# The layout of the gates in DRAM: contiguous for the write or for the read

## What is computed

```python
s = jnp.einsum('thpc,hpkc->thpk', q, sub_keys).astype(jnp.float32)
top_s, top_i = lax.top_k(s, PEER_TOPK)
...
ids = i1 * N_KEYS + i2
g = jax.nn.softmax(best_s, axis=-1)
...
act = jax.nn.gelu(jnp.einsum('td,thkd->thk', xb, ue).astype(jnp.float32), approximate=False)
w = (g * act).astype(xb.dtype)
return jnp.einsum('thk,thkd->td', w, ve)
```

## Time and profile before

| | |
|---|---|
| median of three runs | 2915.62 us (2914.73 to 2916.62) |
| span of the profiled execution | 3018.1 us |
| mean granted TensorE clock | 0.968 |
| PE, DVE, POOL busy | 93%, 77%, 54% |
| DMA, whole span | 685.17 MB, 227 GB/s |

### The profile page before, as it was taken

The page is one execution under the profiler, slowest core; times in us unless marked ns, Lnnn a source line. Parts: engine busy times, 40 slices in busy tenths (PEclk is TensorE's granted clock), DMA queues, the critical chain, the costliest instruction groups (busy, mean ns, idle before and its releaser), DMA issues.

```text
span 3018.1 us, 33873 instructions
## 1 busy us (share of the span) xinstructions
PE 2813.2 (93%) x12016; PEld 2149.1 (71%) x12016; DVE 2333.2 (77%) x3821; ACT 965.7 (32%) x1335; POOL 1617.8 (54%) x1235
## 2 busy tenths in 40 slices
PE   7999699999799999999999999999999999999998
PEld 3546544788588888887777777777777777777776
DVE  2787952588998888886687878878787878788886
ACT  2014232211246656664222222223131313132232
POOL 1999400111023666664476667666666767676640
PEclk9999599999899999999999999999999999999999
DMA  3111010212457999999987888788877888787883
GB/s 120 42 42 56 1 42 1 84 43 84 167 168 233 324 326 335 346 342 361 387 314 264 295 271 295 276 287 291 278 274 265 287 281 288 259 318 278 315 293 147
DMA packets 253977, 685.17 MB, mean 227 GB/s; under 512 B 31984, under 2 KB 97648, under 8 KB 248432
## 3 DMA queue, kind: packets, MB, share of 16 engines
q0 software_dynamic: 104448, 335.81, 31.7%
q1 hardware_dynamic: 83568, 313.65, 29.0%
q10 hardware_dynamic: 65792, 33.56, 3.8%
HBM read 611.60 MB, written 71.30 MB: 226 GB/s over the span
## 4 chain that ended last, share of the span: by engine, by line
PE 42%; DVE 36%; DMA 7%; issue 7%; another core or an unknown queue 3%; DVEq 3%; POOL 1%; ACT 1%; SPq 0%; ACTq 0%; POOLq 0%
PE ps L1625 16%; DVE ps L1240 13%; DMA vring<-in_u_tab,idsA 6%; PE ps L1548 6%; PE ps L1590 5%; DVE hnT L922 4%; PE ps L1476 3%; DVE vl L1299 3%; DVE ul L1214 3%; PE ps L1617 3%; PE ps L1385 2%; DVE hg L1304 2%; DVE wl L1309 2%; DVE lx L1088 2%
## 5 line engine op out<-in xcount | busy, mean ns | idle before, releaser
L555 POOL DMA_INDIRECT vring<-in_v_tab,idsA x512 | 565.0, 1104 | 394.4 <-DVE ps L1240 214.8
L1240 DVE SCALAR_TENSOR_TENSOR ps<-vring,hsel,ps 128x1024 f32<-128x1024 f32 x508 | 652.5, 1284 | 24.6 <-DMA vring<-in_v_tab,idsA 5.8
L530 POOL DMA_INDIRECT hsel<-hidden,idsE x384 | 435.7, 1135 | 125.0 <-issue 114.0
L1625 PE MATMUL ps<-vh,wh 128*128 128x512 f32 x1024 | 410.7, 401 | 74.8 <-DVE wl L1309 66.9
L1625 PE MATMUL ps<-vh,wl 128*128 128x512 f32 x1024 | 409.3, 400 | 4.3 <-issue 4.3
L1617 PE MATMUL ps<-xh,ul 128*128 128x512 f32 x1024 | 406.8, 397 | 4.5 <-issue 4.5
L1617 PE MATMUL ps<-xh,uh 128*128 128x512 f32 x1024 | 406.5, 397 | 4.2 <-issue 3.1
L1617 PE MATMUL ps<-xl,uh 128*128 128x512 f32 x1024 | 405.6, 396 | 4.2 <-issue 3.9
L1625 PE MATMUL ps<-vl,wh 128*128 128x512 f32 x1024 | 407.1, 398 | 2.3 <-issue 2.3
L1316 DVE TENSOR_TENSOR acc<-acc,ps 128x512 f32<-128x512 f32 x256 | 175.0, 684 | 269.6 <-PE ps L1625 162.9
L864 ACT CAST vh<-v_raw 128x1024 fp32r<-128x1024 f32 x128 | 133.9, 1046 | 672.4 <-PE ps L1625 457.3
(11 more groups left out here) (188 smaller groups left out, 4833.3 us busy)
## 6 DMA issues: line engine op xcount, KB each, us to landing
xraw<-in_uX SPq DMA_DIRECT2D x128, 512.0 KB
u_raw<-in_uT SPq DMA_DIRECT2D x128, 512.0 KB
v_raw<-in_v_tab SPq DMA_DIRECT2D x128, 512.0 KB
gates<-gbuf ACTq DMA_DIRECT2D x16, 2048.0 KB
gt<-gates SPq DMA_DIRECT2D x32, 1024.0 KB
hidden<-hst SPq DMA_DIRECT2D x93, 256.0 KB
wqbuf<-in_w_q SPq DMA_DIRECT2D x16, 512.0 KB, 3.4
vring<-in_v_tab,idsA POOLq DMA_INDIRECT x512
```

Of the source, the lines that this page charges most:

```text
L530: nc.gpsimd.indirect_dma_start(out=hsel[:, n, k:k + 1], out_offset=None, in_=hidden_items, in_offset=bass.IndirectOffsetOnAxis(ap=idsE[:, ...
L555: nc.gpsimd.indirect_dma_start(out=vring[q % VS][:, :], out_offset=None, in_=v_rows, in_offset=bass.IndirectOffsetOnAxis(ap=idsA[:, n, k:k ...
L1240: nc.vector.scalar_tensor_tensor(out=bank2(6), in0=vring[slot][:, :], scalar=w, in1=bank2(6), op0=ALU.mult, op1=ALU.add).then_inc(cb_done, 1)
L1625: last = mm(ps[:, 2 + k % 4, :], w[:, c, tt * P:(tt + 1) * P], v[:, c, dh * 512:(dh + 1) * 512], start=c == 0 and w is wh and v is vh, sto ...
```

## The change

The order of the DRAM tensor becomes (set of 32 tokens, partition, block, token). The write of a full `gbuf` is then one run of 16 KB in each partition, and a group's read collects, for each partition, 16 pieces of 4 blocks x 32 tokens, 512 bytes each, that stand 2 MB apart. Bytes, number of transfers, queues, waits and the order of instructions stay as they are, and so does the layout of `gbuf` and `gt`.

```diff
-    gates = nc.dram_tensor("gates", (NG, P, HALF // SUB, GC, SUB), F32, kind="Internal").ap()
+    gates = nc.dram_tensor("gates", (HALF // SUB, P, NKEY, SUB), F32, kind="Internal").ap()
...
             def load_gates(g):
-                sp.dma_start(gt[:, :, :, :], gates[g]).then_inc(g_in, 16)
+                sp.dma_start(gt[:, :, :, :].rearrange("p m c t -> p m (c t)"),
+                             gates[:, :, g * GC:(g + 1) * GC, :].rearrange("m p c t -> p m (c t)")).then_inc(g_in, 16)
...
-                    act.dma_start(gates[:, :, m, :, :].rearrange("g p c t -> p g (c t)"),
-                                  gbuf[m % 2][:, :, :].rearrange("p (g c) t -> p g (c t)", c=GC)).then_inc(gates_out[m % 2], 16)
+                    act.dma_start(gates[m], gbuf[m % 2][:, :, :]).then_inc(gates_out[m % 2], 16)
```

## The result

The changed kernel takes 2948.48 us (median of four, 2944.36 to 2949.25), the kernel before 2916.12 on the same chip. The ratio is 1.0111, 95% interval 1.0097 to 1.0126. It is slower by 32 us, outside the forecast's range and on the other side.

What follows compares the result with a forecast made beforehand. DMA was taken as short in the write stage (98% busy), mostly hidden by PE's `xraw` buffers. - 8.1 - 1 + 1.1 = - 8.0 us gave 2915.6 - 8.0 = 2908 us, own range 2904 to 2914, overall 2888 to 2926.

Steps and rivals of the forecast that it cites:

- The prices: Engine time per piece: 616 ns for a 16 KB write piece, 27.9 ns for a 512-byte read piece.
- What of it reaches the end?: Write stage: of PE's 8.1 us waits for `lx` all are won, of 3.7 for `gbuf` 1; gain 9 us, bounds 0 to 11.8.
- Rival 3: Write stage: the write becomes a burst, `xraw` and gathered rows come 4.9 us late 13 times; + 15 us, 2931; chance 0.13.
- After a burst the engines are free for the others: Write stage, argument against the burst being slower: engines are free until the next write, some 30 us later.
- The sign that the forecast gave for it: Write stage: PE's waits for `lx` would come in runs of one per write if the burst made it slower.
- The extreme case drawn from it: Write stage: a write's eight pieces per engine pass in one turn, 4.9 us with nothing for the other queues.
- 18 us to spare: Later groups' reads: 3.6 us of work takes 9.8 us in place of 8, leaving 18 us before first use.
- Group 0's 1.1 us: Group 0's read, with `hidden` stores behind it that POOL's first gather awaits, is on the path: + 1.1 us (0 to 2.4).
- 2 us more fit in: Group 1's read ends by 1498 us for a use at 1506.23, so 2 us more cause no wait.
- Rival 1: Write stage: PE's wait was not DMA's doing, so only group 0's 1.1 us stays; 2917 (2913 to 2918); chance 0.28.
- rival 2: Write stage: DMA is the bound in the timed runs, so the whole 29 us saving counts; 2887 (or 2899); chance 0.18.
- rival 4: Groups: the read is late above 77 ns a piece, each 10 ns more costing 3.5 us a group; slower; chance 0.05.

Runs made afterwards that it cites:

- the kernel before, again: The kernel before with no edit, profiled a second time: span 2921.6 us, against 3018.1 us in its first profile.
- write's half alone: Against the kernel before: write in 16 KB runs as in the changed kernel, read in 8 KB runs, gates permuted; 2943.38 us, ratio 1.0087.

## Why the prediction was wrong

- **The prices were near.** A 16 KB piece 616 ns, measured 645. DMA share in the stage from 0.98 to about 0.92, measured 0.89. The reads' extra engine time was forecast at 21 to 35 us: queue 1's time went from 30.3% of 16 x 2921.6 us in the kernel before, again, to 31.6% of 16 x 2947.4, 738 us or 46 us of all engines, a third above the upper bound. An issue of the read went from 0.33 to 0.38 us, one of the write from 0.37 to 0.33.
- **The step that failed is "What of it reaches the end?"** It took PE's 8.1 + 3.7 us of waits as what a lighter DMA would give back, 8.1 + 1 in the sum. The lighter DMA did shorten ACT's wait for `xraw` from 990 to 1442, from 100.9 us in the kernel before, again, to 79.0; but in the same stretch PE's wait for `lx` went from 9.3 to 11.3 us, and the wait for `gbuf` from 1.5 to 16.1. The step treats 16 engines as one pool, where less work means earlier data for everybody. What decided was who is served while the write is under way: the write, with 76.5% of the engines for 6 us in the case shown, and SP's and POOL's transfers later. Gain 9 us forecast; loss measured 25 us (write's half alone, 1.0087) and 27 in the changed kernel's stage.
- **Rival 3, given a chance of 0.13, was the mechanism; its 24 us came near by luck.** 4.9 us x 13 x 0.38 = 24 us of waits, less 9 won, + 15. Measured: 13 us of waits more, nothing won, and 13.5 us more of PE's busy time, most of it from the clock, a term that no part of the sum had. Two remarks in it misled. "After a burst the engines are free for the others" is true (DMA share 0.71 from 1080 to 1090 in the changed kernel), but PE had 439.7 busy of 452 us and no room to make a lost wait good. And the names were only half right: `xraw` and gathered rows were named, while the chain runs through `xraw` and ACT's list through the `hidden` stores, whose landing ACT awaits before it copies into `gbuf`. The sign that the forecast gave for it, PE's waits for `lx` in runs of one per write, did not show; the waits for `gbuf` did, behind five of the 16 writes.
- **The rule on turns.** The Trainium skill (DMA: Bandwidth & Descriptors, "Queues, rings and completion order") has an engine take turns between queues by packets. The runs agree in direction: 22.1, 16.3, 14.2 and 11.5 us to land with 512-byte, 2, 4 and 16 KB pieces. The extreme case drawn from it is not far off: with a write in one turn nothing would have been left for the others for 4.9 us, and they had 27% of the engines' time (16.8 + 10.5) in the 6 us in which nearly all of the write shown passed. With one 4 KB piece of each other queue between, it would have been 38% over 8 us.
- **The read: two groups right, one wrong.** For the later groups 9.8 us in place of 8 was forecast, and 18 us to spare. The same group's read in the changed kernel, 2048 packets between 512 bytes and 2 KB from 2014 to 2025, 11 us:

```profile
DMA packets 2948, 3.80 MB, mean 345 GB/s; under 512 B 235, under 2 KB 2283, under 8 KB 2945
...
q0 software_dynamic: 803, 2.44, 61.1%
q1 hardware_dynamic: 2142, 1.32, 41.9%
```

  No product of these 30 groups waited. Group 0's 1.1 us for the `hidden` stores: POOL's wait went from 7.8 us (before, again) to 9.8 in the changed kernel, within the bounds (engines shared by half make 2.2 us, not the 2.4 given as the upper one). Group 1's "2 us more fit in" was wrong in what the read would take: it landed 24.1 us after its issue in the kernel before, again, and 38.1 us after it in the changed one. There the 2048 pieces pass between 1520 and 1541:

```profile
q0 software_dynamic: 1866, 5.79, 74.3%
q1 hardware_dynamic: 2346, 2.06, 29.5%
```

  With 74.3% of the engines at POOL's queue, 3.6 / 0.257 = 14 us would have been the estimate by the forecast's own method, and even that is short of the 21 measured; the share of another group, 63.4%, had been carried over. The wait is 8.0 us, and 5 to 7 us is what the groups are longer in every kernel that reads in pieces with SP's list as it was (1477.0 to 1479.3 against 1472.0).
- **The rule on pitch.** The Trainium skill (same page, "Latency and other measured facts") has copies with rows 2 MiB apart slower than at 512 KiB. An estimate from the queue's time is 30 ns for a read's piece, 2 MB from the next: the reads' 33.6 MB at 26.6 KB/us were 1261 us, with 738 more 2.0 ms for 65,536 pieces. That is between the forecast's 27.9 and the 35 estimated by the rule; it decided nothing.
- **Rival 1** falls with the sign, **rival 2** with the second profile of the kernel before, **rival 4** holds for one group only.

## What to carry to other kernels

A background transfer that nobody waits for was better thin here. In pieces of 512 bytes or 2 KB the write took more engine time than in pieces of 16 KB (4.0 and 3.1% of the engines against 2.8%), and the kernel was faster; four issues in place of one, spread over the time that it has, made it a little faster again. Before counting saved DMA time as a gain, ask whose transfers share the engines with it, which of them a busy engine waits for, and whether that engine has room to make up a wait. Take the share of the engines that a transfer will get from the very place where it is to run; the first group's start had another mixture than the groups after it.

## What the runs showed of the hardware

Over the write stage PE's waits of 13.3 us more came with 13.5 us more of busy time for nearly the same matmuls. In the changed kernel PE waited 3.77 us for `lx` up to 1224.80 and then ran the first matmuls at about half the pace (start us, us):

```profile
1225.39 0.63 PE L1590 MATMUL ps<-lx,xh 128*128 128x512 f32 x1
1225.82 0.63 PE L1590 MATMUL ps<-hx,xl 128*128 128x512 f32 x1
...
1230.26 0.40 PE L1590 MATMUL ps<-lx,xh 128*128 128x512 f32 x1
1230.49 0.39 PE L1590 MATMUL ps<-hx,xl 128*128 128x512 f32 x1
```

Starts are 0.43 us apart behind the wait and 0.23 from 1230 on. The granted clock in the 5 us behind the wait is 0.50, the lower of the two levels (1.2 and 2.4 GHz), with PE busy all the time:

```profile
1224.80:1229.80 5.00, 5.00 (x12) 3.94 (x13) 4.91 (x6) 0.00 (x0) 2.47 (x2) 0.50 0.77 236
```

For the 5.45 us wait shown above, up to 1114.16, the granted clock from 1110 to 1120 is 0.83: the lower level for a part of that time.

Two profiles of one kernel, the kernel before, differ by 96 us of span (3018.1 and 2921.6) with the medians unchanged; the difference lies in one stage. A span that stands 3% above the median of the runs should be taken again before its rows are trusted.
